# GpSimd's two sums left to TensorE: four turned products stored, twice as many output matmuls, a third row in the phase table

## What is computed

```python
for layer in range(2):
    proj = rms_norm(x, norm_mix[layer]) @ w_in[layer]       # q, k, v, u, two gates
    a = diff_attention(rotary(q), rotary(k), v, lam)        # 4 heads, two score maps each, softmax(s0) - lam*softmax(s1)
    a = rms_norm(a, attn_subln[layer]) * (1.0 - lam_init)
    s = gelu(s5_bidirectional(u, ...))                      # 32 groups of 16 channels, 64 complex states, 2 directions
    s = s * sigmoid(s @ w_glu[layer])
    merged = gates[0] * (a @ w_branch[layer, 0]) + gates[1] * (s @ w_branch[layer, 1])
    x = x + merged @ w_out[layer]
    hn = rms_norm(x, norm_ffn[layer])
    x = x + (swiglu(hn, ...) if layer == 0 else moe_swiglu(hn, ...))   # top 2 of 8 experts
return rms_norm(x, norm_final)
```

## Time and profile before

| | us |
|---|---|
| three runs | 1575.27, 1578.36, 1578.65 |
| median | 1578.36 |
| the profiled execution | 1573.4 |
| its span, first to last instruction | 1571.4 |

### The profile page before, as it was taken

The page is one execution under the profiler, slowest core; times in us unless marked ns, Lnnn a source line. Parts: engine busy times, 40 slices in busy tenths (PEclk is TensorE's granted clock), DMA queues, the critical chain, the costliest instruction groups (busy, mean ns, idle before and its releaser), DMA issues.

```text
span 1571.4 us, 24603 instructions
## 1 busy us (share of the span) xinstructions
PE 1437.1 (91%) x8917; PEld 1179.0 (75%) x8917; DVE 1199.8 (76%) x1290; ACT 890.3 (57%) x950; POOL 323.6 (21%) x328
## 2 busy tenths in 40 slices
PE   4697969999998979698899999999999999999996
PEld 3585748788887867477788887888888888888884
DVE  6969947655446569466788998889988898888985
ACT  4243444644434433444576776767767677676774
POOL 3737841998000068300000000000000000000000
PEclk9798979999999989898999999999999999999998
DMA  9332234556544422186599999999999999999970
GB/s 264 108 94 84 82 94 151 183 187 199 188 160 161 136 68 95 40 296 214 197 365 345 347 362 321 362 334 350 362 320 362 332 350 364 328 350 334 350 270 27
DMA packets 273555, 374.68 MB, mean 238 GB/s; under 512 B 17360, under 2 KB 220496, under 8 KB 273360
## 3 DMA queue, kind: packets, MB, share of 16 engines
q1 hardware_dynamic: 265568, 366.46, 69.0%
q10 hardware_dynamic: 6640, 4.16, 1.1%
q0 software_dynamic: 1280, 3.15, 1.0%
HBM read 371.63 MB, written 1.05 MB: 237 GB/s over the span
## 4 chain that ended last, share of the span: by engine, by line
PE 75%; DVE 13%; issue 5%; ACT 5%; DMA 1%; POOL 1%; ACTq 0%; POOLq 0%; DVEq 0%
PE bank L533 73%; DVE lo L1322 4%; ACT hi L984 2%; PE bank L551 1%; PE bank L914 1%; DVE raw L1407 1%; DVE at_lo L1754 1%; DVE at_lo L1723 1%; DVE qk L1440 1%; DMA areg<-in_norm_mix_dram 1%; DVE raw L1387 0%; DVE raw L1388 0%; DVE raw L356 0%; DVE bank L1398 0%; DVE raw L1397 0%
## 5 line engine op out<-in xcount | busy, mean ns | idle before, releaser
L1322 DVE TENSOR_TENSOR lo<-raw,hi 128x2048 fp32r<-128x2048 f32 x347 | 810.7, 2341 | 164.3 <-ACT hi L984 154.1
L984 ACT ACTIVATE hi<-raw 128x2048 fp32r<-128x2048 f32 x347 | 662.8, 1914 | 119.7 <-PE bank L533 113.2
L533 PE MATMUL bank<-hi,at_hi 128*128 128x512 f32 x1280 | 519.5, 406 | 36.5 <-DVE areg L1374 12.0
L533 PE MATMUL bank<-hi,at_lo 128*128 128x512 f32 x1280 | 505.0, 395 | 0.0
L533 PE MATMUL bank<-lo,at_hi 128*128 128x512 f32 x1280 | 504.7, 394 | 0.0
L533 PEld LDWEIGHTS bank<-hi,at_hi 128*128 128x128 f32 x1280 | 244.1, 191 | 91.1 <-issue 24.9
L533 PEld LDWEIGHTS bank<-hi,at_lo 128*128 128x128 f32 x1280 | 243.5, 190 | 52.6
L533 PEld LDWEIGHTS bank<-lo,at_hi 128*128 128x128 f32 x1280 | 244.4, 191 | 46.4
L533 PE MATMUL bank<-hi,ht_hi 128*128 128x512 f32 x440 | 172.2, 391 | 4.5 <-DVE ht_lo L1655 3.5
L533 PE MATMUL bank<-hi,ht_lo 128*128 128x512 f32 x440 | 171.3, 389 | 0.0
L533 PE MATMUL bank<-lo,ht_hi 128*128 128x512 f32 x440 | 171.3, 389 | 0.0
(11 more groups left out here) (261 smaller groups left out, 1170.1 us busy)
## 6 DMA issues: line engine op xcount, KB each, us to landing
raw<-in_moe_w_dram SPq DMA_DIRECT2D x528, 512.0 KB, 5.4
raw<-in_ffn_w_dram SPq DMA_DIRECT2D x66, 512.0 KB, 4.2
raw<-in_w_in_dram SPq DMA_DIRECT2D x64, 512.0 KB, 4.5
raw<-in_w_branch_dram SPq DMA_DIRECT2D x16, 512.0 KB, 4.2
raw<-in_w_out_dram SPq DMA_DIRECT2D x16, 512.0 KB, 4.7
raw<-in_w_glu_dram SPq DMA_DIRECT2D x4, 512.0 KB, 4.3
xres<-in_x_dram SPq DMA_DIRECT2D x2, 512.0 KB, 6.2
areg<-in_norm_mix_dram ACTq DMA_DIRECT2D x2, 512.0 KB, 6.4
```

The lines of the kernel that those rows point to most:

```text
L533: return pe.matmul(o, a, b, start=start, stop=stop)
L984: act.activation(hi[:, slot, :], src, ACT.Copy).then_inc(hi_ready, 1)
L1322: tt(lo[:, slot, :], src, hi[:, slot, :].bitcast(f32), SUB).then_inc(lo_ready, 1)
```

## The change

- `turn_forward` stores the four products themselves: `xst` gets a leading axis `part` of two, and the difference and the sum are gone. For the sign of the difference the table `wtab` has a third row, the negated sines. `s5_out` multiplies both parts with the same C matrix into the same place, 36 matmuls a duo instead of 20.
- `wtab`: GpSimd makes half of each row (four products of half the width, two sums), and ScalarE fills the rest by mirrored copies, together with a table of decays (`scan_tables`, five copies, in turn s ahead of the high part of tile 10+s). `phases` is gone from VectorE.
- `s5_scan`: the third row makes the two half-wide sums one full-wide sum, and the decay table with zeros at the seams makes eight scans of 64 two of 256.
- Attention: q is scaled with the negated factor when it is turned, so `row_max` is a single minimum. The exponential is written in place in PSUM, and `scale_second` and `weights` read it there. A score bank is therefore free only when `weights` is done.
- `inner`: two banks instead of four, zero fills first, the skip diagonal by TensorE, matrices of two halves side by side; then two copies by ScalarE. `inner_diagonal` goes ahead of the splits of tiles 8 and 9. The transfers to `cbm` are now sixteen half ones issued by SP after the load of tile 12; `kc` lies in the space of `areg`, so GpSimd waits only for `kc_full`, and ScalarE waits for the transfers once, in `head_back(0)`.
- `phasors`: the tables have 16 and 2 columns instead of 16 and 4.
- Router: the logits are done in two halves, the first ahead of the last norm transposes; the two sums use the banks PY; the overflow table is made for three places at once; the gather and its high and low parts are signalled by halves.

```diff
-        php = [area(TMP + 1024, 256), area(TMP + 1280, 256), php_last[:, :]]
-        zs = area(TMP + 2048, 512).rearrange("p (r c) -> p r c", r=2)
-        po1 = area(TMP + 2560, 512).rearrange("p (r c) -> p r c", r=2)
-        po2 = area(TMP + 3072, 512).rearrange("p (r c) -> p r c", r=2)
+        wtab = [area(LOOP + 768 * i, 768).rearrange("p (r c) -> p r c", r=3) for i in range(2)]
+        decay = area(LOOP + 1536, 256).rearrange("p (j c) -> p j c", j=4)
+        xst = [area(LOOP + 2816 + 1040 * i, 1040).rearrange("p (t r e c) -> p t r e c", t=2, r=2, e=2) for i in range(2)]
...
+            elif name[1] == "sc":
+                free_at[name] = (w_ready, 8 * name[0] + name[2] + 1)
...
+            def inner_moves(l):
+
+                sp.wait_ge(kc_ready, 2 * (l + 1))
+                for half in range(2):
+                    for g in range(2):
+                        for i in range(4):
+                            r0, s0 = 64 * g + GC * i, 64 * g + 32 * half
+                            sp.dma_start(cbm[r0:r0 + GC, 8 * half:8 * half + 8, :],
+                                         kc[s0:s0 + GC, :, GC * (3 - i):GC * (3 - i) + 64]).then_inc(cbm_in, 16)
...
-                                states = xs[rows, r, e, 0:64] if d == 0 else xs[rows, r, e, 66:130]
-                                mm(o[rows, :], cblk[rows, r, q, 4 * d:4 * d + 4, :].rearrange("p i h -> p (i h)"), states,
-                                   d + r == 0, False)
+                                for part in range(2):
+                                    states = xs[rows, part, r, e, 0:64] if d == 0 else xs[rows, part, r, e, 66:130]
+                                    mm(o[rows, :], cblk[rows, r, q, 4 * d:4 * d + 4, :].rearrange("p i h -> p (i h)"), states,
+                                       d + r + part == 0, False)
...
             def inner(l):
 
+                if l == 0:
+                    pe.wait_ge(loads, 32)
+                for bank in PY:
+                    mm(bank[:, 0:448], ident, cst[:, C_TRI:C_TRI + 1].broadcast_to([P, 448]), True, False)
+                pe.wait_ge(kdiag_ready, l + 1)
                 pe.wait_ge(b_part, l + 1)
                 pe.wait_ge(c_ready, l + 1)
...
+            def scan_tables(l, m):
+
+                n = DUOS * l + m
+                if n > 0:
+                    act.wait_ge(zs_ready, n)
+                act.activation(decay[:, :, 1:64],
+                               par[:, RAD4, 32 * l + 4 * m:32 * l + 4 * m + 4].unsqueeze(2).broadcast_to([P, 4, 63]),
+                               ACT.Copy).then_inc(decay_ready, 1)
+                act.wait_ge(wtab_half, n + 1)
+                for r in range(2):
+                    upper, lower = halves_of(m, r)
+                    act.activation(lower, upper[:, :, ::-1], ACT.Copy, scale=1.0 if r == 0 else -1.0)
+                minus = halves_of(m, 2)
+                act.activation(minus[0], upper, ACT.Copy, scale=-1.0)
+                act.activation(minus[1], upper[:, :, ::-1], ACT.Copy).then_inc(wtab_ready, 1)
...
-                inner_moves(l)
+                scan_tables(l, 0)
                 if l == 0:
                     act.wait_ge(lam_ready, 1)
                     act.activation(col(LEXP, 4), col(LSUM, 4), ACT.Exp).then_inc(lam_exp, 1)
                 for s in range(8):
+                    if s < 7:
+                        scan_tables(l, s + 1)
                     split_static(t + 10 + s)
...
-                own.step(tt(rot2, v[:, ::-1, :], w[:, 1:2, :].broadcast_to([P, 2, 256]), MUL))
+                own.step(tt(rot2, v[:, ::-1, :], w[:, 1:3, :], MUL))
                 own.step(tt(v, v, w[:, 0:1, :].broadcast_to([P, 2, 256]), MUL))
-                own.step(tt(v[:, 0, :], v[:, 0, :], rot2[:, 0, :], ADD))
-                own.step(tt(v[:, 1, :], v[:, 1, :], rot2[:, 1, :], SUB))
+                own.step(tt(v, v, rot2, ADD))
                 if n > 0:
-                    dve.wait_ge(zs_used, n)
+                    dve.wait_ge(states_ready, n)
+                dve.wait_ge(decay_ready, n + 1)
                 for r in range(2):
-                    for j in range(4):
-                        part = slice(64 * j, 64 * j + 64)
-                        c = 32 * l + 4 * m + j
-                        last = dve.tensor_tensor_scan(zs[:, r, part], par[:, RAD4, c:c + 1].broadcast_to([P, 64]),
-                                                      v[:, r, part], 0.0, MUL, ADD)
+                    last = dve.tensor_tensor_scan(zs[:, r, :], decay.rearrange("p j c -> p (j c)"), v[:, r, :], 0.0, MUL, ADD)
                 last.then_inc(zs_ready, 1)
...
+                inner_diagonal(l)
                 split_static(t + 8)
                 split_static(t + 9)
-                inner_diagonal(l)
...
-                f1, f2 = (a.rearrange("p r (e c) -> p r e c", e=2) for a in (po1, po2))
-                tt(xs[:, 0, :, 1:129], f1[:, 0], f2[:, 0], SUB)
-                tt(xs[:, 1, :, 1:129], f1[:, 1], f2[:, 1], ADD).then_inc(states_ready, 1)
+                for part, src, turn in ((0, z, None), (1, z[:, ::-1], w[:, 2:0:-1])):
+                    for d in range(2):
+                        dst = xs[:, part, :, :, 1:65] if d == 0 else xs[:, part, :, :, 128:64:-1]
+                        by = w[:, 0:1, :, d, :].broadcast_to([P, 2, 2, 64]) if turn is None else turn[:, :, :, d, :]
+                        last = tt(dst, src[:, :, :, d, :], by, MUL)
+                last.then_inc(states_ready, 1)
...
-                pool.wait_ge(cbm_in, KC_LOADS * (l + 1))
+                pool.wait_ge(kc_full, 2 * (l + 1))
```

More of the change, by code:

```diff
@@ L67, in mixer_turns @@
         names += [(l, "h", g) for g in GROUPS]
-    names += ["router", "pos"]
     return {name: n for n, name in enumerate(names)}
@@ L881, in _ @@
             mm(bank[:, 16:24], ones, sel[:, 0, :], True, False)
-            mm(bank[:, 16:24], ones, sel[:, 1, :], False, True).then_inc(tr_full, 1)
+            mm(bank[:, 16:24], ones, sel[:, 1, :], False, True).then_inc(pos_full, 1)
             def gather():
@@ L1682, in _ @@
                 ts(xn[:, th, :], xn[:, th, :], col(RI + th), None, MUL).then_inc(xn_scaled, 1)
-            bank = wait_turn(dve, "router")
+            dve.wait_ge(logits_full, 1)
+            bank = PY[0]
             sums = bank[:, 0:32].rearrange("p (t i e) -> p t i e", t=2, i=2)
             own.step(dve.tensor_copy(r_tmp, sums[:, :, 0, :]))
-            tt(r_logit, r_tmp, sums[:, :, 1, :], ADD).then_inc(tr_free[TURN["router"] % 2], 1)
-            wait_read(dve, "router")
+            own.step(tt(r_logit, r_tmp, sums[:, :, 1, :], ADD))
             for th in range(TH):
@@ L1710, in _ @@
             own.step(ts(cols[:, 0, :, 0:NE], r_pos, -1.0, None, ADD))
-            ts(r_over, bank[:, 16:24], float(P), None, ALU.is_gt).then_inc(tr_free[TURN["pos"] % 2], 1)
-            wait_read(dve, "pos")
+            own.step(ts(r_over, bank[:, 16:24], float(P), None, ALU.is_gt))
             def places():
```

252 lines of the change are left out of this document (122 added, 130 removed).

## The result

| | before | after |
|---|---|---|
| median of the runs made side by side, us | 1578.12 (4 runs, 1575.27 to 1578.65) | 1550.14 (4 runs, 1549.79 to 1552.75) |
| profiled execution, us | 1573.4 | 1549.79 |
| its span, us | 1571.4 | 1547.6 |

What follows compares the result with a forecast made beforehand. TensorE's own order was taken to bound the mixer loop, with waits around it. 6.5 + 4.2 + 9.0 + 4.3 - 7.3 - 1.0 = 15.7 us off 1573.4, plus 5.0 to the median: 1562.7 us, range 1551 to 1575.

Steps and rivals of the forecast that it cites:

- The floor of the loop: Mixer loop: TensorE's own order sets six turns at 63.5 us before, 69.7 after; loss 7.3 us over both layers.
- The scans: VectorE in the loop: two 256-wide scans replace eight short ones of 1.54 us, taken at 1.1 us for both.
- The last turn: End of each mixer loop: GpSimd wait of 4.24 us and half clock go, longer output matmuls added; gain 4.5 us a layer.
- The first turn of layer 1: Before layer 1's first weight transpose: SP issues the transfers, GpSimd's clearing no longer waits; transpose 6.5 us earlier.
- The first turn of layer 0: Before layer 0's first weight transpose: exponential no longer behind transfers, but inner products wait for the diagonal; gain 4.2 us.
- The inner products: Within-chunk matrices on TensorE: 272 wider records instead of 384, taking 6.0 us by records or 8.7 at 32 ns each.
- The gather: First expert: gather split into halves lets TensorE go straight on, 2.4 us; nothing in later blocks.
- The clock: TensorE's half clock after waits: two shorter waits remain in each first turn; 1.0 us taken back in all.
- A: Rival, chance 0.12: ScalarE's tables bound the loop; twelve turns lose 11 us more than forecast, 1573 us.
- B: Rival, chance 0.07: slower than before; scores wait for banks released by the weighting, plus half clock; 1598 us.
- D: Rival, chance 0.07: SP's sixteen transfers eat the first-turn gain, 12 us less, and the tail stays bound; near 1575 us.
- C: Rival, chance 0.10: added matmuls overlap, inner products at record price, first turn at full clock; 25 us gain, 1553 us.

Runs made afterwards that it cites:

- sums_back: The changed kernel with GpSimd's difference and sum put back, 20 output matmuls a duo instead of 36: 1548.2 us, ratio to before 0.9828.
- tile_early: The changed kernel with tile 10 of each mixer split ahead of the inner products instead of in the loop's first turn: 1542.4 us.
- inner_pairs: The changed kernel with the same 256 inner-product records a layer in another order, alternating between two TensorE tiles instead of four: 1550.7 us.
- gather_whole: The changed kernel with the first expert's gather signalled whole instead of by halves, as in the kernel before: 1553.1 us.
- before_sp: The kernel before with the eight transfers of the within-chunk matrices issued by SP instead of ScalarE: 1567.9 us, ratio 0.9962.
- tables_twice: The changed kernel with ScalarE's four table copies of each duo done twice, the second four into unused space: 1553.5 us.
- moves_act: The changed kernel with its sixteen transfers issued by ScalarE, ahead of the first duo's tables, instead of SP: 1571.8 us.
- The headline part, alone or undone: GpSimd's sums dropped for 36 output matmuls a duo: alone on the kernel before, 1568.1 us, ratio 0.9942; undone in the changed kernel, 1548.2 us.
- six_sums: The changed kernel with turned weights copied before gates, tile 10 split early, and GpSimd sums in place for duos 1 to 6 only: 1533.6 us.
- three_in_one: The changed kernel with GpSimd's sums back, turned weights copied before the gates and tile 10 split early: 1530.6 us, ratio to before 0.9721.

## Why the prediction was off in size

The sign and the places were right, the size too small: 15.7 us forecast against the profiled execution, 23.8 measured between the spans. The terms that were too small are the inner products, the first turn of layer 1 and the gather, and the step from the profiled execution to the median was wrong.

- **The added matmuls**: 1.03 us a turn forecast, 3.30 - 2.31 = 0.99 measured. Right.
- **The floor of the loop** was sized wrong twice, and the errors cancelled. Six turns between the transposes hold five `s5_in`, not six (the last of them has no next duo), so the floors are near 62.6 and 68.7, not 63.5 and 69.7; sums_back (63.2 to 63.5) and tile_early (68.4) show both. What was not TensorE's own in six turns of before was thus 3.4, not 2.5. In their place after pays 2.3 and 1.5 us of half clock (70.71 and 69.96 against the 68.42 of tile_early; inner_pairs and gather_whole pay 2.3 in both layers). Forecast loss with the clock 8.3, measured 8.6.
- **The scans**: two of 256 took 1.26 us, the eight took 1.53; I had 1.1. The saving is 0.27 us. The rule of the Trainium skill ("DVE: opcode table, instruction layouts, handler registers and perf-mode slots", section 6) is that the scan runs at half throughput. The trace agrees in so far as six scans fewer saved little. The estimate of about 0.4 that I had worked out from the rule is the saving of my own 1.1 as well, so the two were never apart.
- **The last turn**: 4.5 forecast, 4.9 and 4.9. Its three terms were right; the half microsecond set aside for a remaining wait was not needed.
- **The first turn of layer 1**: 6.5 forecast, 8.9. The path was right (tables, scan, tables, high part, low part, minimum, scan, weighting: TensorE's wait ends on the weighting), its terms too dear. Table copies took 1.1 us for five, not 1.7, twice on the path; the low part 2.3, not 2.75, though GpSimd was at work beside it (two phase products in 2.89 us, which take 0.76 elsewhere); and the first tables started 17.2 us behind the keys (547.37), not 18.7, since the inner products were shorter.
- **The first turn of layer 0**: 4.2 forecast, 6.0, less the 1.3 by which the stretch ahead of it was longer. The diagonal let the inner products begin 3.9 us later than before, as estimated (4 to 5), but they took 5.8 us, so that the B powers came 0.6 us later (10.65 us behind the keys instead of 10.05), not 2. before_sp shows the gain itself to be the transfers' (6.0).
- **The inner products** were the worst price: 6.0 to 8.7 us for 272 records. In layer 1 these took 4.5, the 256 of them shown above 4.2. The range went down to the record price of before, and the truth lay beneath it.
- **The gather**: 2.4 forecast, 4.8. I counted the wait and not the clock behind it, though the earlier trace rows hold it: 24 matmuls in 7.36 us, where the same take 5.5 at full clock. gather_whole gives it back. VectorE's rank chain did become half as long (2.8 us instead of 5.8), but gather_whole, which keeps it short, has the same wait of 2.50: the chain did not hold TensorE.
- **The logits**: 2.0 forecast, 3.0 for the whole stretch from the last turn to the gather; no run undoes them alone. With the gather's 2.4 they make 4.4, not the 4.3 of the sum.
- **The clock**: 1.0 us forecast for the new waits, 3.8 measured (2.3 and 1.5, behind the waits that end the first turns). I had taken as the price of a wait of 2.10 and shorter waits as nearly free. The Trainium skill's section on gaps ("TensorE: Matmul & The Clock Gate", "Why this matters for your kernels") warns of longer gaps only, and here the trace decides: 1.66 us of wait were followed by half clock, 1.05 in the loop and 1.67 in the experts' first block were not.
- **The median above the profiled execution**: I added 5.0 to the sum. It was no property of the kernel: after's median stands 0.35 above its own, and before itself had medians of 1574.5 to 1575.1 in the later comparisons, over runs that spread by 9 us. Without that step the forecast would have been 1557.7, 7.6 too high instead of 12.6.
- **The rivals**: A is excluded by tables_twice; its 11 us don't follow from its own turns either, which make 7 (6 x 0.8 and 6 x 0.35). B did not show: no turn of after waits at its scores. D did not either: TensorE waits for none of SP's transfers, and the last turns are 4.9 us shorter. moves_act ends near D's 1575, but by ScalarE's issuing and not by SP's. C came nearest. It named cheap inner products, which were cheaper still; its other two reasons were not so (the added matmuls took 0.99, and the first turn's waits cost the clock).

What I had not asked is which part earns the gain. The headline part, alone or undone, moves the time by 2.5 (spans) to 9 us (ratio) around before and not measurably around after. The gain is for the most part that of its companions: transfers moved from ScalarE to SP (before_sp), the gather's halves (gather_whole) and, read from the traces and undone by no run, inner products in fewer records and the logits in halves.

Left open: what makes the inner products cheap, which waits cost the clock and which do not, and which of two instructions, VectorE's split or the one of GpSimd beside it, is the longer for it.

## What to carry to other kernels

Work moved from an engine that is off the path to TensorE cost nearly its full length in every turn here and paid only at the ends, where TensorE waited; count both before calling it a gain. A wait of TensorE that you remove or add can have a second price, the matmuls at half clock behind it, and it is in the same rows: compare their time with that of the same matmuls elsewhere. A transfer's issue is work of the engine that issues it: sixteen a layer on ScalarE's path cost 22 us over the two layers, and TensorE waited for none of them when SP issued them.

## What the hardware showed

- After a wait of 1.66 us behind 104 small records and two scores TensorE ran busy at a granted clock of 0.64 over 3.5 us, after one of 3.05 us at the same place of layer 0 at 0.50 over 4.6 us. Behind full tiles, waits of 1.05 us (in the loop) and of 1.67 us (742.62) left it at full clock. A wait of 1.29 us, behind 40 small records and not full tiles, was followed by half clock too (six_sums).
- A GpSimd sum of 128 x 256 took 0.72 to 0.75 us alone and 2.66 to 2.87 beside VectorE's split of a tile (sums_back, three_in_one). In six_sums the splits of layer 0's loop took 2.47 to 3.23 us, against 2.29 to 2.58 in after.
- Weighting with one operand in PSUM took VectorE 0.48 us, in all sixteen turns. With both operands in SBUF it took 0.78 to 1.01 in the loop of before, with GpSimd at work beside it, and 0.48 behind the last turn, without.
- Records of 64 x 16 by 64 columns took 15 to 16 ns each in a run of 128, in either order of their tiles.
